# y stores on two queues in the first layer, and another order and a halved end of the experts in the last

## The reference, cut to what matters

```python
def hier_moe(h, gw, gb, ew, eb, w_gu, w_down):      # 16 experts in 4 groups
    g_sel = jnp.argmax(g_logits, axis=-1)           # top group
    top_v, top_i = lax.top_k(e_in, TOP_K_IN_GROUP)  # two experts in it
    ...
    for e in range(N_EXPERTS):
        gu = tok @ w_gu[e]                          # 1024 x 1024
        act = jax.nn.silu(gu[:, :D_EXPERT]) * gu[:, D_EXPERT:]
        y = y + combine[:, e:e + 1] * (act @ w_down[e])   # 512 x 1024
    ...
        x = x + mx[5] * rms_norm(fx, norm_g[layer, 3])    # in reference(), behind it
```

## Time and profile before

| | |
|---|---|
| median of 3 runs | 1138.76 us (1137.25 to 1141.07) |
| the profiled execution, its own time | 1147.01 us |
| its span | 1144.8 us |
| PE busy | 956.8 us (84%) |
| DVE, ACT, POOL busy | 391.1, 280.5, 140.3 us |
| DMA | 313.51 MB, 274 GB/s over the span |
| queue q1 (SP, weights) | 279.19 MB, 60.2% of 16 engines' span |
| queue q10 (ScalarE, y stores) | 7.92 MB, 14564 packets |
| queue q0 (GpSimd, gathers and rows) | 25.25 MB, 7536 packets |

### The profile page before, as it was taken

How to read it: one execution, slowest core, us unless ns; L and a number is a source line. 1 busy time by engine, 2 the same in 40 slices (tenths; PEclk the granted TensorE clock), 3 DMA queues, 4 the chain that set the end, 5 groups by cost and what they waited for, 6 DMA issues and landing times. The chain is left out here.

```text
span 1144.8 us, 24422 instructions
## 1 busy us (share of the span) xinstructions
PE 956.8 (84%) x9652; PEld 597.8 (52%) x9653; DVE 391.1 (34%) x1003; ACT 280.5 (25%) x756; POOL 140.3 (12%) x198
## 2 busy tenths in 40 slices
PE   4989989899999599987788179998998698797684
...
GB/s 376 354 278 99 147 74 221 199 215 213 74 164 149 346 306 413 424 423 425 417 323 423 315 373 189 220 163 58 112 74 160 373 306 426 425 426 428 428 357 56
DMA packets 55844, 313.51 MB, mean 274 GB/s; under 512 B 12106, under 2 KB 19908, under 8 KB 37204
## 3 DMA queue, kind: packets, MB, share of 16 engines
q1 hardware_dynamic: 33664, 279.19, 60.2%
q0 software_dynamic: 7536, 25.25, 6.3%
q10 hardware_dynamic: 14564, 7.92, 2.3%
...
## 5 line engine op out<-in xcount | busy, mean ns | idle before, releaser
L556 PE MATMUL psum<-hT,weights 128*128 128x512 f32 (+1 forms) x336 | 120.8, 519 | 3.6 <-ACT lat L1196 2.1
L1007 PE MATMUL psum<-weights,lat 128*32 128x256 f32 x1568 | 92.3, 386 | 17.4 <-issue 7.1
L921 PE MATMUL psum<-weights,lat 128*32 128x256 f32 x992 | 70.1, 438 | 29.4 <-issue 15.9
L556 PEld LDWEIGHTS psum<-hT,weights 128*128 128x128 f32 x336 | 64.8, 194 | 56.2 <-issue 47.7
L1007 PEld LDWEIGHTS psum<-weights,lat 128*32 128x32 f32 x1568 | 60.0, 111 | 47.3 <-issue 24.5
L1668 DVE TENSOR_REDUCE st<-psum 128x1 f32<-128x512 f32 (+1 forms) x96 | 56.7, 599 | 49.8 <-PE psum L672 21.2
L921 PEld LDWEIGHTS psum<-weights,lat 128*32 128x32 f32 x992 | 39.2, 123 | 57.7 <-issue 44.2
L1289 ACT ACTIVATE R<-psum,st 128x512 f32<-128x512 f32 (+1 forms) x78 | 48.0, 616 | 81.7 <-DVE st L1668 48.6
L1825 DVE STREAM_TRANSPOSE lat<-lat 128x256 f32<-128x256 f32 x41 | 18.3, 446 | 139.3 <-PE psum L1007 130.3
L788 PE MATMUL psum<-weights,hT 128*128 128x512 f32 x144 | 65.2, 608 | 0.0
L1020 PE MATMUL psum<-weights,lat 128*32 128x256 f32 x832 | 51.7, 387 | 6.9 <-ACT lat L1394 3.4
...
## 6 DMA issues: line engine op xcount, KB each, us to landing
...
```

Source lines behind the costliest of these rows:

```text
L556: mm = nc.tensor.matmul(t[:, lo:hi], w[:, k, col:col + P], hT[:, k, lo:hi], start=(k == 0), stop=(k == KD - 1))
L921: mm = nc.tensor.matmul(gu_ps[BLK * j:BLK * j + BLK, 0:256], xgT[:, k, :], w[:, k % 4, j, :, :], start=(k == 0), stop=(k == KD - 1), skip_ ...
L1007: mm = nc.tensor.matmul(gu_ps[BLK * j:BLK * j + BLK, 0:256], xgT[:, k, :], w[:, k % 4, j, :, :], start=(k == 0), stop=(k == KD - 1), skip_ ...
```

## The change: what it does

**First layer.** ScalarE issues two of the four stores of a block; GpSimd issues the other two from its own queue, behind its gather, with a semaphore of its own (`y_rest`), and ScalarE waits for both semaphores before it writes a buffer again. The writing of zeros to y_rows at the start is cut into eight transfers instead of two, of the same bytes.

**Last layer, order.** The first four experts keep their places; of the others, the last two that have one block go to the end. With these inputs that is the order 0 to 11, 14, 15, 12, 13 (before: 0 to 15). VectorE computes this order: eight operations ahead of the slot positions, and eight more plus the writing of `tab`, now behind the weights (`by_position`, `tables`).

**Last layer, end.** The last expert's down piece is loaded in two transfers, by half columns; its down product, the copy, the adding of rows and the squares go by halves (`last_expert`). Its predecessor's down product goes ahead of its gate/up product. The combine multiplies by the gate row while the norm is still being worked out, and then scales and adds x in one operation per tile (the last tile in two halves, each with its own store). GpSimd no longer adds.

The diff, cut to its core:

```diff
+FIXED, LATE = 4, 2
+    put("first", np.tile(16384.0 * np.maximum(FIXED - np.arange(16), 0) + 15.0 - np.arange(16), (P, 1)))
...
+                def down_half(done, place, half):
+
+                    if half == 0:
+                        pe.wait_ge(y_copied, done)
+                        pe.sem_inc(sem("pe_hold"), 1)
+                        pe.wait_ge(actT_ready, done)
+                    for b in range(4):
+                        for j in (2 * half, 2 * half + 1):
+                            mm = nc.tensor.matmul(y_ps[BLK * j:BLK * j + BLK, 0:256], actT[:, b, :], w_dn[place][:, b, j * 256:(j + 1) * 256],
+                                                  start=(b == 0), stop=(b == 3), skip_group_check=True)
+                    mm.then_inc(y_done if half else sem("half_down"), 1)
+
+                def add_half(count, half):
+
+                    if half == 0:
+                        pe.wait_ge(sem("hot_weighted"), count)
+                        pe.sem_inc(sem("pe_hold"), 1)
+                        pe.wait_ge(sem("half_copied"), 1)
+                    else:
+                        pe.wait_ge(y_copied, count)
+                    for tt in range(2):
+                        for j in (2 * half, 2 * half + 1):
+                            mm = nc.tensor.matmul(psum[:, B_OUT[j], tt * 256:(tt + 1) * 256], hot_weight[BLK * j:BLK * j + BLK, tt * P:(tt + 1) * P],
+                                                  y_sb[0][BLK * j:BLK * j + BLK, :], start=False, stop=True, skip_group_check=True)
+                    mm.then_inc(sem("rows_added" if half else "half_added"), 1)
+
+                def last_expert(triple, place):
+
+                    n_blocks = pe.value_load(tabs[L][0:1, triple * 3 + T_NB + place:triple * 3 + T_NB + place + 1], min_val=1, max_val=MORE + 1)
+                    start = pe.value_load(tabs[L][0:1, triple * 3 + T_START + place:triple * 3 + T_START + place + 1], min_val=0, max_val=MAXBLK)
+                    total = pe.value_load(tabs[L][0:1, T_TOTAL:T_TOTAL + 1], min_val=N_EXP, max_val=MAXBLK)
+                    landed = (triple + (uses(place) + 1)) * 16
+                    down(start, (place + 2) % 3)
+                    add_rows(start)
+                    gate_up(start, place, (landed_lo(L, triple, place), landed))
+                    select(start + 1)
+                    with pe.If(n_blocks > 1):
+                        pe.wait_ge(sem(f"w_dn{place}"), landed)
+                        pe.wait_ge(sem("w_dn_rest"), 16)
+                        with pe.Fori(start + 1, start + n_blocks) as g:
+                            block(g, place, place)
+                    add_rows(total)
+                    pe.wait_ge(sem(f"w_dn{place}"), landed)
+                    down_half(total, place, 0)
+                    add_half(total + 1, 0)
+                    pe.wait_ge(sem("w_dn_rest"), 16)
+                    down_half(total, place, 1)
+                    add_half(total + 1, 1)
...
-                expert(N_EXP // 3, 0)
-                total = pe.value_load(tabs[L][0:1, T_TOTAL:T_TOTAL + 1], min_val=N_EXP, max_val=MAXBLK)
-                down(total, 0)
-                add_rows(total)
-                add_rows(total + 1)
+                last_expert(N_EXP // 3, 0)
...
-                    act.wait_ge(sem(f"y_stored{place}{L}"), ((n + 3) >> 2) * (16 * QUADS))
+                    for key in ("y_stored", "y_rest"):
+                        act.wait_ge(sem(f"{key}{place}{L}"), ((n + 3) >> 2) * (8 * QUADS))
                     a(y_out_sb[place], psum[:, 3, 0:256], ACT.Copy).then_inc(y_copied, 1)
                     act.wait_ge(y_copied, n + 1)
-                    for j in range(QUADS):
+                    for j in range(QUADS // 2):
                         act.dma_start(y_rows[ds((n if row is None else row) * BLK - BLK, BLK), j * 256:(j + 1) * 256], y_out_sb[place][BLK * j:BLK * j + BLK, :])\
                             .then_inc(sem(f"y_stored{place}{L}"), 16)
...
+                act.wait_ge(sem("half_down"), 1)
+                act.wait_ge(sem("rows_added"), total)
+                a(y_sb[0][0:64, :], psum[0:64, B_Y, 0:256], ACT.Copy).then_inc(sem("half_copied"), 1)
+                act.wait_ge(sem("half_added"), 1)
+                act.sem_inc(sem("hold_act"), 1)
+                half_squares(0)
+                act.wait_ge(y_done, total)
+                a(y_sb[0][64:128, :], psum[64:128, B_Y, 0:256], ACT.Copy).then_inc(y_copied, 1)
+                act.wait_ge(*at("y_sq", L, 0))
+                a(rs[:, 23, 0:2], rs[:, 20, 0:2], ACT.Identity, scale=1.0 / D, bias=C("eps")).then_inc(*mark(S, ("y_part", L)))
                 act.wait_ge(sem("rows_added"), total + 1)
                 act.sem_inc(sem("hold_act"), 1)
-
-            def combine_last():
-                S, L = "act_comb1", 1
+                half_squares(1)
...
+                start_of = start32[:, 0:16]
+                if L:
+                    start_of = order_start
+                    step(ts(one_block, nb32[:, 1:17], float(BLK), None, ALU.is_equal))
+                    step(nc.vector.tensor_tensor_scan(order_pos, ones[:, 0:16], one_block, 0.0, ALU.mult, ALU.add))
+                    step(ts(order_start, order_pos, order_pos[:, 15:16], 1.0 - LATE, ALU.subtract, ALU.is_ge))
+                    step(stt(order_key, order_start, -64.0, one_block, ALU.mult, ALU.mult))
+                    step(tt_(order_key, order_key, C("first"), ALU.add))
+                    step(tt_(ahead_of, order_key.unsqueeze(1).to_broadcast([P, 16, 16]), order_key.unsqueeze(2).to_broadcast([P, 16, 16]), ALU.is_gt))
+                    step(tt_(ahead_sum, ahead_of, nb32[:, 1:17].unsqueeze(1).to_broadcast([P, 16, 16]), ALU.mult))
+                    step(red(order_start, ahead_sum, AX.X, ALU.add))
                 place = vals[:, 0, 0:ne].rearrange("p (t e) -> p t e", t=nt)
-                step(tt_(place, t[:, 0:ne].rearrange("p (e t) -> p t e", t=nt), start32[:, 0:16].unsqueeze(1).to_broadcast([P, nt, 16]), ALU.add), ("read", "rk", L))
+                step(tt_(place, t[:, 0:ne].rearrange("p (e t) -> p t e", t=nt), start_of.unsqueeze(1).to_broadcast([P, nt, 16]), ALU.add), ("read", "rk", L))
...
+                def by_position():
+
+                    step(red(order_pos, ahead_of, AX.X, ALU.add))
+                    step(tt_(ahead_of, order_pos.unsqueeze(1).to_broadcast([P, 16, 16]), C("count")[:, 0:16].unsqueeze(2).to_broadcast([P, 16, 16]), ALU.is_equal))
+                    step(tt_(ahead_sum, ahead_of, nb32[:, 1:17].unsqueeze(1).to_broadcast([P, 16, 16]), ALU.mult))
+                    step(red(nb32[:, 1:17], ahead_sum, AX.X, ALU.add))
+                    step(nc.vector.tensor_tensor_scan(start32[:, :], ones[:, 0:17], nb32[:, :], 0.0, ALU.mult, ALU.add))
+                    step(tt_(ahead_sum, ahead_of, C("count")[:, 0:16].unsqueeze(1).to_broadcast([P, 16, 16]), ALU.mult))
+                    step(red(order_id, ahead_sum, AX.X, ALU.add))
+                    ts(tabs[L][:, T_ID:T_ID + 16], order_id, 1.0, None, ALU.mult)
...
+                    by_position()
+                    tables()
...
+                for half in range(2):
+                    v.wait_ge(*at("y_sq", L, half))
+                    dst = y_pair[:, :, half * 512:half * 512 + 512].rearrange("p t (j c) -> p j t c", j=2)
+                    sums = psum[:, 4 + 2 * half:6 + 2 * half, :].rearrange("p j (t c) -> p j t c", t=2)
+                    gates = gate_last[:, half * 512:half * 512 + 512].rearrange("p (j c) -> p j c", j=2).unsqueeze(2).to_broadcast([P, 2, 2, 256])
+                    tt_(dst, sums, gates, ALU.mult).then_inc(*mark(S, ("y_gated", L, half)))
+                v.wait_ge(*at("y_gated", L, 1))
                 v.wait_ge(*at("y_rstd", L))
-                for tt in range(2):
-                    dst = ya[tt].rearrange("p (j c) -> p j c", j=4)
-                    stt(dst, psum[:, 4:8, tt * 256:(tt + 1) * 256], rs[:, 22, tt:tt + 1], gate3_row[0].rearrange("p (j c) -> p j c", j=4),
-                        ALU.mult, ALU.mult).then_inc(*mark(S, ("y_norm", L, tt)))
-                v.wait_ge(*at("y_norm", L, 1))
-                tt_(ya[1], ya[1], x_tok[:, 1, :], ALU.add).then_inc(*mark(S, ("x", L, 2, 1)))
+                for tt, lo, hi in ((0, 0, D), (1, 0, D // 2), (1, D // 2, D)):
+                    stt(ya[tt][:, lo:hi], ya[tt][:, lo:hi], rs[:, 22, tt:tt + 1], x_tok[:, tt, lo:hi], ALU.mult, ALU.add)\
+                        .then_inc(*mark(S, ("x", L, 2, tt, hi)))
...
-                with g_.Fori(0, pairs) as pair:
-                    for par in range(2):
-
-                        g_.wait_ge(x_ready, pair * 2 + (par + 1))
-                        g_.sem_inc(sem("hold"), 1)
-                        gather(pair * 2 + (par + 2), par)
+
+                def next_gather(g, i, column=None):
+                    g_.wait_ge(x_ready, g + 1)
+                    g_.sem_inc(sem("hold"), 1)
+                    gather(g + 2, i % 2, column=column)
+
```

(20 more changed lines are left out.)

91 lines of the change are left out of this document (57 added, 34 removed).

## The result

The changed kernel takes **1133.84 us** (median of 16 runs, 1129.56 to 1137.57) against 1139.88 us for the kernel before on the same chip: a ratio of 0.9948, 95% interval 0.9928 to 0.9968, so faster by 6 us. The forecast was 1122.8 us with a range of 1117 to 1130.5: the sign is right, the size is not, and the time lies outside the range.

The account below looks back on a forecast made before the run. Bound: the DMA weight stream, stalled by store waits in the first layer, then TensorE's chain at the last layer's end. First layer -6.5 and last layer -9.5 sum to -16.0 us, from 1138.76 to 1122.8 us, range 1117 to 1130.5.

Parts of the forecast that it names:

- Gain: the idle DMA of the stretch, 7.0 us: First layer, 570 to 584 us: stores on two queues recover idle DMA time, 7.0 us (5.6 us by its share).
- +0.5 for the gate rows: End of first layer: gate rows, queued behind last stores and ahead of y gathers, cost 0.5 us (between 0 and 2.5).
- +4.2 us: Last layer's routing: added VectorE work makes the second gate/up and all landings 4.2 us later (bounds 3 and 6).
- Gain 6.7 us, net of the routing: Last layer: with experts 14 and 15 moved ahead, the last gate/up ends at 1115.2 instead of 1121.9, 6.7 us sooner.
- 20.1 us, a gain of 2.8: Last layer, from last gate/up's end to kernel's end: 20.1 us instead of 22.9, gain 2.8 (bounds 0 and 4).
- the store and end: Final part of the tail: store and end take 5.5 us, a smaller last store than before.
- adding of the block before to 4.6: Tail: adding of the block before is done 4.6 us after the last gate/up's end, behind the one-hot matrix at 3.3.
- first half down 5.6: Tail: first half of the last down product is done 5.6 us after the last gate/up's end.
- The end of the second addition, forecast at 9.4: Tail: adding behind the second copy (8.7) is done 9.4 us after the last gate/up's end.
- rival 3: First layer: GpSimd's queue becomes the bound, gathers land late; 1137 us at its upper price, 1144 at 6.7 us a block; chance 0.05.
- Rival 1: First layer gives nothing: second queue adds no turn, or GpSimd's queue needs 6.1 us a block; 1129.3 us, chance 0.17.
- Rival 2: Last layer gives half: routing costs 6 us, the end runs at 1.2 GHz, tail's 2.8 us gone; 1127.4 us, chance 0.15.

## Why the prediction was wrong

**First layer, "Gain: the idle DMA of the stretch, 7.0 us", and +0.5 for the gate rows.** The mechanism holds: no wait of the y copy, no dip, the stream ahead. Its size was 4.3 us, and the stream itself, by the wait for its last hi piece, came 4.4 us sooner. The share of the earlier trace rows, which the prediction gave beside the rate, says 5.6 us, not 7.0: the engines were busy for 0.60 of the stretch while they moved half of the full rate. Over all sixteen profiles, from 175 to 205 us after the first gate/up, the share is 0.80 to 0.85 with one queue and 1.01 to 1.02 with two, which is 5.5 us. Where the last microsecond of these goes isn't shown. TensorE's idle time of 5 to 7 us at the last expert and its products at 1.2 GHz, for which the sum had nothing, cost nothing on average. The first gather comes 255.2 - 249.1 = 6.1 us after the last down matmul's start with one queue and 250.9 - 244.2 = 6.7 with two, the +0.5 of the forecast, though for another reason: GpSimd waits for the last stores.

**Routing, "+4.2 us".** 3.4 us by the second gate/up product, 2.5 by the whole stage of the kernel that pays it and has no use of it, 0.7 by its median. Mis-sized by about two, to the good.

**"Gain 6.7 us, net of the routing".** 4.9 us by C. The base was a long profile: its own C was 222.8, and from that the gain is 6.8. So the step was read rightly from rows that stood 2 us too high, and taking the excess of 8 us off at the end, as the forecast did, doesn't mend a difference between stages.

**The tail, "20.1 us, a gain of 2.8".** This step failed: D grew by 3.1 us where it should have shrunk by 2.6 (the other 0.2 is the store and end, 5.5 for 5.7, which came to 3.5). The one-hot matrix was ready at 1109.34 - 1106.35 = 3.0 us (forecast 3.3). From there on: "adding of the block before to 4.6" came to 7.05 us (1113.40), since TensorE stood behind the skipped loop; "first half down 5.6" gave half the matmuls half the time, and came to 10.6 (1116.95): a half takes as long as the whole, and this one ran at 1.2 GHz. The four column groups of a block go to four quarters of the array (128*32 in the rows: 128 rows by 32 columns) and the rows show them side by side: 32 matmuls of four groups in 1.93 us, 16 of two groups in 1.92. Cutting by columns cut the parallelism, not the time. The end of the second addition, forecast at 9.4, came at 15.8; from there to the last VectorE instruction the sum had 5.2 and the profile has 5.3, so the whole error lies ahead of it. The bound from below was 0, for slow products alone; a longer chain was not among the bounds, nor a rival.

**The sum.** -16.0 forecast. By the cuts -4.3 - 4.9 + 3.1 - 2.2 = -8.3 us, and 0.5 less between the span and the execution's own time (2.2 before, 1.7 after): -8.8. The two measurements gave -6.0 and -5.3 us by medians, -5.9 and -7.1 by ratios, with intervals that reach to -8.2 and -10.0. What divides the cuts from the medians, 2 us or so, is not settled. The 2.0 us of the end that the forecast did not have lie in all of these, by luck and not by its working: without them it would have missed by as much more. Also, the median of before that the forecast started from, 1138.76, stood 1.1 us below that of 16 runs.

**The rivals.** All but rival 3 put the time below the measured one. Rival 1 (a second queue adds nothing) and rival 3 (GpSimd's queue becomes the bound) fall: two stores and a gather fit, with the y copies of an expert's blocks 5.18 us apart in the stretch where they were 7.38, and no wait for a gather. The Trainium skill's rule (DMA: Bandwidth & Descriptors, Rules for kernel authors) says that spreading over SP, ACT and GpSimd doesn't help bandwidth and only saves issue time. On bandwidth it agrees, 424 GB/s from 530 to 550 us in both kernels; that nothing but issue time is saved is contradicted here for small stores beside large loads, whose waits went, with A 4.3 us shorter. Rival 2, half of the last layer, is nearest in its mechanism, by its tail and not by its routing; rival 1's number, 1129.3, is nearer.
